# Sparse, block and memory attention: values stationary by column halves, softmax divided ahead of the turn, a new order

## What is computed

```python
# sparse layer: 12 heads, one k and v of 64 columns each for "selected" and "window"
k_cmp = gelu(blocks(k) @ w1) @ w2             # 15 blocks of 32 tokens, stride 16: [15, 2048] @ [2048, 256]; the same for v
o_c = softmax(q @ k_cmp + bias) @ v_cmp
o_s = softmax(q @ k_slc + bias, causal) @ v_slc   # 4 blocks of 64 tokens, top 16: all are selected
o_w = softmax(q @ k_win + bias, causal) @ v_win   # the window is 512: all tokens
o = gate_c * o_c + gate_s * o_s + gate_w * o_w
# block layer: 12 heads with k and v of their own; blocks of 256 tokens, so one block
o = softmax(q @ k + bias, causal) @ v
# both: 4 heads of memory attention (256 memory rows), then
mix = concat(o, o_mem) @ w_out
x = layer_norm(ALPHA * x + mix)
```

## Time and profile before

| | us |
|---|---|
| median of 3 runs | 988.98 (988.08 to 990.57) |
| the profiled execution | 987.35 |
| its span on the core | 985.5 |
| TensorE busy, of the span | 935.0 (95%) |
| VectorE busy | 607.0 (62%) |
| ScalarE busy | 470.5 (48%) |

### The profile page before, as it was taken

How to read it: one execution, slowest core, us unless ns; L and a number is a source line. 1 busy time by engine, 2 the same in 40 slices (tenths; PEclk the granted TensorE clock), 3 DMA queues, 4 the chain that set the end, 5 groups by cost and what they waited for, 6 DMA issues and landing times.

```text
span 985.5 us, 15654 instructions
## 1 busy us (share of the span) xinstructions
PE 935.0 (95%) x6226; PEld 835.4 (85%) x6226; DVE 607.0 (62%) x1108; ACT 470.5 (48%) x833; POOL 37.5 (4%) x72
## 2 busy tenths in 40 slices
PE   8999999699999899889999999998999999999997
PEld 8888978588978777867799999987987889999995
DVE  5669565556566525765786766566444677756565
ACT  5464364355574335652454444434554354444440
POOL 1005100100000100000000000000000000000000
PEclk9999999889999799999999999999999999999999
DMA  8835334264534334212555555546233365555551
GB/s 311 289 129 183 129 108 151 78 219 160 161 107 155 122 117 160 95 43 86 192 173 184 190 180 189 179 171 224 97 108 107 128 203 188 189 174 189 191 192 43
DMA packets 45508, 155.14 MB, mean 157 GB/s; under 512 B 5404, under 2 KB 8060, under 8 KB 45436
## 3 DMA queue, kind: packets, MB, share of 16 engines
q1 hardware_dynamic: 41840, 145.98, 43.2%
q10 hardware_dynamic: 3596, 8.16, 2.9%
HBM read 152.78 MB, written 1.34 MB: 156 GB/s over the span
## 4 chain that ended last, share of the span: by engine, by line
PE 82%; DVE 9%; ACT 6%; issue 2%; POOL 1%; DMA 1%; DVEq 0%; ACTq 0%
PE ps L1933 12%; PE ps L1922 8%; PE ps L1921 8%; PE ps L1920 8%; PE ps L749 6%; PE ps L656 5%; PE ps L657 5%; PE ps L658 5%; PE ps L672 4%; PE ps L861 4%; PE ps L674 4%; PE ps L673 4%; PE ps L828 2%; PE ps L836 2%; ACT sm L896 2%
## 5 line engine op out<-in xcount | busy, mean ns | idle before, releaser
L623 DVE TENSOR_TENSOR wlo<-raw,whi 128x1024 fp32r<-128x1024 f32 (+1 forms) x263 | 313.2, 1215 | 47.8 <-ACT whi L617 47.4
L617 ACT ACTIVATE whi<-raw 128x1024 fp32r<-128x1024 f32 (+1 forms) x263 | 271.4, 1047 | 126.2 <-DMA raw<-in_ws 46.8
L1920 PE MATMUL ps<-thi,whi 128*128 128x256 f32 x640 | 181.2, 283 | 0.0
L1922 PE MATMUL ps<-thi,wlo 128*128 128x256 f32 x640 | 181.1, 283 | 0.0
L1921 PE MATMUL ps<-tlo,whi 128*128 128x256 f32 x640 | 181.1, 283 | 0.0
L1921 PEld LDWEIGHTS ps<-tlo,whi 128*128 128x128 f32 x640 | 122.8, 192 | 0.7
L1920 PEld LDWEIGHTS ps<-thi,whi 128*128 128x128 f32 x640 | 122.8, 192 | 0.7
L1922 PEld LDWEIGHTS ps<-thi,wlo 128*128 128x128 f32 x640 | 122.8, 192 | 0.0
L656 PE MATMUL ps<-thi,whi 128*128 128x256 f32 (+1 forms) x416 | 121.5, 292 | 0.4 <-ACT arena L1542 0.4
L657 PE MATMUL ps<-tlo,whi 128*128 128x256 f32 (+1 forms) x416 | 118.3, 284 | 0.0
L658 PE MATMUL ps<-thi,wlo 128*128 128x256 f32 (+1 forms) x416 | 118.2, 284 | 0.0
(11 more groups left out here) (251 smaller groups left out, 1315.1 us busy)
## 6 DMA issues: line engine op xcount, KB each, us to landing
raw<-in_ws SPq DMA_DIRECT2D x264, 512.0 KB, 4.0
vecs<-in_vecs ACTq DMA_DIRECT2D x12, 512.0 KB, 6.1
raw<-in_ws SPq DMA_DIRECT2D x4, 384.0 KB, 3.9
tb<-brow ACTq DMA_DIRECT2D x8, 192.0 KB, 4.5
rows<-in_mem SPq DMA_DIRECT2D x2, 512.0 KB, 4.2
x<-in_x SPq DMA_DIRECT2D x1, 1024.0 KB, 9.5
out<-x SPq DMA_DIRECT2D x4, 256.0 KB, 2.0
tb<-in_decay SPq DMA_DIRECT2D x1, 768.0 KB, 8.8
```

Source lines behind the costliest of these rows:

```text
L617: a.i.activation(whi[:, j % NSPLIT, 0:n], raw[:, u % NRAW, 0:n], ACT.Copy).then_inc(*a.sig("hi", u))
L623: d.i.tensor_tensor(wlo[:, j, 0:n], raw[:, u % NRAW, 0:n], whi[:, j, 0:n].bitcast(F), ALU.subtract).then_inc(*d.sig("lo", u))
L1920: p.i.matmul(o, wh[:, k, :], thi[:, k, :], start=k == 0, stop=False)
L1922: mm = p.i.matmul(o, wl[:, k, :], thi[:, k, :], start=False, stop=k == 7)
```

## The change

- `w1`: its eight units move to the end of the plan and out of the ring `raw`; ScalarE issues their loads (step `w1load`) into six buffers of their own. The four contraction tiles of a step go to four quarters of 32 output partitions (`blk` widened from 15 to 32 columns); `comp 1` adds the quarters up and turns them with a matmul against `quarters`, and the gelu comes after it.
- Groups of the sparse, block and memory attention get a `mul` step (`dve_scale`): VectorE divides the probabilities by their sum, and multiplies them by the gates, before they are turned; `pe_turn` waits for it.
- `val` (`pe_val_columns`): the value (64 columns) is stationary, the turned probabilities (128 columns) move, side 0 writes output partitions 0 to 63 and side 1 64 to 127. In the sparse stage both branches, and the compressed one by a full matmul, add up in PSUM. The output is already the transposed one that the projection takes.
- `fin` is now the split into high and low part (`act_out`, `dve_out`); `mix`, `cmpo`, and the divisions and sums of `dve_fin` for these groups are gone. `pe_project` waits for `out_lo` of the group.
- New orders of both lists, sparse groups with rows 0 ahead of rows 1; the block stage's half-full group moves from the last place to heads 0 to 3.

```diff
-    w1 = [(nm, k) for nm in "kv" for k in range(4)]
-    for t in range(6):
-        for nm, k in w1[2 * t:2 * t + 2] if t < 3 else ():
-            unit(f"a_w1{nm}", f"a_cmp_w1_{nm}_2", span(0, 256), span(4 * k, 4), split=False)
-        if t == 3:
-            for nm, k in w1[6:8]:
-                unit(f"a_w1{nm}", f"a_cmp_w1_{nm}_2", span(0, 256), span(4 * k, 4), split=False)
-        tiles("a_q", a, span(0, 768), only=(t,))
...
+    for nm in "kv":
+        for k in range(4):
+            unit(f"a_w1{nm}", f"a_cmp_w1_{nm}_2", span(0, 256), span(4 * k, 4), split=False)
...
+    at = ODD.index(("proj", "o", 4, 0))
+    ODD[at:at] = [("w1load", i) for i in range(4)]
...
+        nsa += [nsa_group(0, 4 * i, 4), nsa_group(1, 4 * i, 2), nsa_group(1, 4 * i + 2, 2)]
...
+    NSA = [
+        ("chunk", "a_v", 0, 0), ("chunk", "a_v", 1, 0), ("T", 5, 1), ("w1load", 4), ("chunk", "a_v", 0, 1), ("chunk", "a_v", 1, 1),
+        ("tile", "a_c", 0), ("blocks",), ("tile", "a_c", 1), ("w1", "k", 0), ("tile", "a_qm", 0), ("w1", "k", 1), ("w1load", 5),
+        ("w1", "k", 2), ("w1load", 6), ("tile", "a_qm", 1), ("w1", "k", 3), ("w1load", 7), ("log", m0), ("w1", "v", 0),
+        ("tile", "a_q", 0), ("w1", "v", 1), ("tile", "a_q", 1), ("mul", m0), ("w1", "v", 2), ("w1", "v", 3), ("comp", 0), ("log", m1),
+        ("turn", m0, 0), ("tile", "a_q", 2), ("log", n0), ("mul", m1), ("comp", 1), ("tile", "a_q", 3), ("turn", m0, 1), ("comp", 2),
+        ("turn", m1, 0), ("turn", m1, 1), ("val", m0), ("fin", m0), ("mul", n0), ("tile", "a_q", 4), ("log", n1), ("turn", n0, 0),
+        ("turn", n0, 1), ("comp", 3), ("log", n2), ("tile", "a_q", 5), ("val", m1), ("mul", n1), ("turn", n1, 0), ("mul", n2),
+        ("fin", m1), ("turn", n1, 1), ("log", n3), ("cmp",), ("turn", n2, 0), ("add_x", "a", 0), ("add_x", "a", 1), ("cmp2",),
+        ("proj", "a", 0, 0), ("log", n4), ("cmpt", 0), ("proj", "a", 1, 0), ("log", n5), ("mul", n3), ("proj", "a", 0, 1),
+        ("turn", n2, 1), ("val", n0), ("proj", "a", 1, 1), ("fin", n0), ("proj", "a", 2, 0), ("turn", n3, 0), ("cmpt", 1), ("mul", n4),
+        ("turn", n3, 1), ("val", n1), ("fin", n1), ("val", n2), ("fin", n2), ("turn", n4, 0), ("log", n6), ("mul", n5),
+        ("turn", n4, 1), ("val", n3), ("proj", "a", 3, 0), ("turn", n5, 0), ("proj", "a", 2, 1), ("fin", n3), ("mul", n6),
+        ("proj", "a", 3, 1), ("turn", n5, 1), ("val", n4), ("log", n7), ("fin", n4), ("proj", "a", 4, 0), ("turn", n6, 0), ("log", n8),
+        ("mul", n7), ("proj", "a", 4, 1), ("turn", n6, 1), ("val", n5), ("fin", n5), ("proj", "a", 5, 0), ("val", n6), ("mul", n8),
+        ("fin", n6), ("proj", "a", 5, 1), ("turn", n7, 0), ("turn", n7, 1), ("proj", "a", 6, 0), ("turn", n8, 0), ("turn", n8, 1),
+        ("val", n7), ("proj", "a", 7, 0), ("fin", n7), ("proj", "a", 6, 1), ("norm", "a", 0), ("val", n8), ("fin", n8), ("T", 7, 0),
+        ("proj", "a", 7, 1), ("norm", "a", 1),
+    ]
...
+    moba = [group("moba", 1, evens(0, 4), 0, 4, 0), group("moba", 0, evens(0, 4), 0, 4, 0), group("moba", 1, evens(4, 4), 4, 4, 256),
+            group("moba", 0, evens(4, 8), 4, 8, 256), group("moba", 1, evens(8, 4), 8, 4, 512)]
...
+    after = {2: [("log", m0)], 3: [("log", m1), ("mul", m0)], 4: turn_of(m0) + [("mul", m1)], 5: turn_of(m1) + done(m0) + [("log", g2)],
+             6: done(m1) + [("log", g3), ("mul", g2)], 7: turn_of(g2) + [("mul", g3)], 8: done(g2) + turn_of(g3), 9: done(g3) + [("log", g4)],
+             10: [("mul", g4)], 11: turn_of(g4)}
     MOBA += woven(slots, *[(k, [v]) for k, v in after.items()])
-    MOBA += [("mix", "b", 2), ("add_x", "b", 0), ("log", g6), ("add_x", "b", 1), ("proj", "b", 0, 0), ("proj", "b", 0, 1)] + turn_of(g5)
-    MOBA += [("proj", "b", 1, 0), ("proj", "b", 1, 1)] + done(g5) + turn_of(g6) + [("proj", "b", 2, 0), ("proj", "b", 2, 1)] + done(g6)
-    MOBA += [("proj", "b", 3, 0), ("mix", "b", 3), ("proj", "b", 3, 1)]
+    MOBA += [("log", g5), ("add_x", "b", 0), ("add_x", "b", 1)] + done(g4) + proj("b", 0, 0) + proj("b", 0, 1) + [("log", g6), ("mul", g5)]
+    MOBA += proj("b", 1, 0) + proj("b", 1, 1) + [("turn", g5, 0), ("mul", g6)] + proj("b", 2, 0) + [("turn", g5, 1)] + proj("b", 2, 1) + done(g5)
+    MOBA += turn_of(g6) + proj("b", 3, 0) + proj("b", 3, 1) + done(g6)
...
+    def act_w1_load(a, i):
+
+        if i < 4:
+            a.wait_ge("mix_t", "o", 3)
+        elif i < 6:
+            a.wait_ge("xw", "o", 1, 1)
+        else:
+            a.wait_ge("w1", w1_units[i - 6])
+        at = plan[w1_units[i]]["at"]
+        a.i.dma_start(w1_bufs[i % 6], inp["ws"][at:at + P * UNIT].rearrange("(p n) -> p n", p=P)).then_inc(*a.sig(f"w1raw{i}", "all", by=16))
...
+        if (s, n, q) in gives:
+            p.wait_ge("out_lo", gives[s, n, q].g)
+        else:
+            p.wait_ge("mix_lo", s, n // 2)
...
-        p.wait_ge("mul" if g.kind == "diff" else "exp", g.g)
+        p.wait_ge("mul" if g.scaled else "exp", g.g)
...
+    def pe_val_columns(p, g):
+
+        if g.kind == "nsa":
+            p.wait_ge("pcT", g.q)
+        p.fill(g.out, ("out_hi", g.g), ("out_lo", g.g))
+        z = 2 if g.kind == "nsa" else 1
+        for c in range(len(g.sides[0])):
+            o = c // z * P
+            for y in range(g.nb):
+                k = (c * g.nb + y) * P
+                for s in range(2):
+                    mm = p.i.matmul(ps[64 * s:64 * s + 64, g.out, o:o + P], value(g, s, c, y), g.pts[s][:, k:k + P],
+                                    start=c % z == 0 and y == 0, stop=g.kind != "nsa" and y == g.nb - 1)
+            if g.kind == "nsa" and c % 2:
+                h = g.h0 + c - 1
+                mm = p.i.matmul(ps[:, g.out, o:o + P], N["vbd"][:, h % 4:h % 4 + 2, :].rearrange("p h d -> p (h d)"),
+                                N["pcT"][:, g.q, h // 4 * P:h // 4 * P + P], start=False, stop=True)
+        mm.then_inc(*p.sig("val", g.g))
+
+    def out_tiles(s, g):
+
+        n0 = MIX_ORDER[s].index(g.at // P)
+        for a, b in ((n0, min(n0 + g.n // 2, 4)), (max(n0, 4), n0 + g.n // 2)):
+            if a < b:
+                hi, lo, n = mixed(a)
+                yield ps[:, g.out, (a - n0) * P:(b - n0) * P].rearrange("p (k n) -> p k n", n=P), [
+                    v[:, n:n + b - a, g.q * P:g.q * P + P] for v in (hi, lo)]
+
+    def act_out(a, s, g):
+        a.wait_ge("val", g.g)
+        for src, (hi, _) in out_tiles(s, g):
+            last = a.i.activation(hi, src, ACT.Copy)
+        last.then_inc(*a.sig("out_hi", g.g))
+
+    def dve_out(d, s, g):
+        d.wait_ge("out_hi", g.g)
+        for src, (hi, lo) in out_tiles(s, g):
+            last = d.i.tensor_tensor(lo, src, hi.bitcast(F), ALU.subtract)
+        last.then_inc(*d.sig("out_lo", g.g))
...
+    def dve_scale(d, g):
+
+        n, W = len(g.sides[0]), g.W
+        d.wait_ge("exp", g.g)
+        d.i.reciprocal(g.l, g.l).then_inc(*d.sig("dve"))
+        d.wait_ge("dve")
+        if g.kind == "nsa":
+            d.wait_ge("gate", g.q)
+            gates = N["gte"][:, g.q, 3 * g.h0:3 * g.h0 + 3 * g.n].rearrange("p (i s c) -> p s i c", s=2, c=3)[:, :, :, 1:3]
+            l = g.l.rearrange("p (s i z) -> p s i z", s=2, z=2)
+            d.i.tensor_tensor(l, l, gates, ALU.mult).then_inc(*d.sig("dve"))
+            d.wait_ge("dve")
+        for s in range(2):
+            v = g.slots[s][:, 0:n * W].rearrange("p (c w) -> p c w", c=n)
+            mu = d.i.tensor_tensor(v, v, g.l[:, s * n:s * n + n].unsqueeze(2).to_broadcast([P, n, W]), ALU.mult)
+        mu.then_inc(*d.sig("mul", g.g))
...
-                p.wait_ge(f"raw{u % NRAW}", u)
-                wv = raw[:, u % NRAW, 0:1024].rearrange("p (k n) -> p k n", k=4)
+                i = w1_units.index(u)
+                p.wait_ge(f"w1raw{i}", "all")
+                wv = w1_bufs[i % 6].rearrange("p (k n) -> p k n", k=4)
                 for kl in range(4):
-                    kt = 4 * a[1] + kl
-                    mm = p.i.matmul(ps[0:15, 2, T * z:T * z + T], N["blk"][:, z, kt, :], wv[:, kl, :], start=kt == 0, stop=kt == 15)
+                    mm = p.i.matmul(ps[32 * kl:32 * kl + 32, 2, T * z:T * z + T], N["blk"][:, z, 4 * a[1] + kl, :], wv[:, kl, :],
+                                    start=a[1] == 0, stop=a[1] == 3)
                 mm.then_inc(*p.sig("w1", u))
             elif what == "comp" and a[0] == 1:
...
+                p.wait_ge("quarters", 0)
+                p.fill(2, ("hid", 0))
                 for y in range(4):
-                    t = p.i.transpose(ps[:, 2, 16 * y:16 * y + 15], N["hrow"][0:15, y * P:y * P + P], ident[0:15, 0:15])
-                t.then_inc(*p.sig("hidt", 0))
+                    mm = p.i.matmul(ps[:, 2, 16 * y:16 * y + 16], N["hrow"][:, y * P:y * P + P], quarters[:, 0:16], start=True, stop=True)
+                mm.then_inc(*p.sig("hidt", 0))
```

More of the change, by code:

```diff
@@ L294, in _build @@
     nhalf = sb("nhalf", [P, 8])
+    quarters = sb("quarters", [P, 32])
     AW = 9728
@@ L370, in _build @@
     split_no = {u: j for j, u in enumerate(split_units)}
```

(43 more changed lines are left out.)

151 lines of the change are left out of this document (60 added, 91 removed).

## The result

| | before | changed |
|---|---|---|
| median, us | 988.68 (988.08 to 990.57) | 964.16 (961.63 to 967.14) |
| ratio | | 0.975 [0.972, 0.978] |
| span of the profiled execution | 985.5 | 959.8 |

A forecast was written before the change was run, and what follows sets the result against it. TensorE was taken to bound both stages. Sparse stage - 18.4 us of work and + 4.2 of idle, block stage - 5.8, together - 20.0: span 985.5 to 965.5, median 969.0 us, range 956 to 985.

The forecast's parts named there:

- Overlap of column halves and quarters: Values and w1: matmuls run side by side; values save 8.4 us (sparse) and 4.9 us (block), w1 9.4 us.
- Rival (c): Values and w1: 32-bit halves by columns don't overlap, so both cost more; 992.5 us at its middle; chance 0.13.
- (d): Values and w1: two at a time where four are meant, pairs gain half; 979 us; chance 0.16 together with Rival (b).
- The drain at a change of mode: TensorE, value and w1 steps: changing between whole and halved array costs about 0.2 us; if free, about 5 us better.
- Work taken off: Sparse stage, TensorE: values - 8.4, w1 - 9.4, mix - 1.7, comp 1 + 0.5, branch sum + 0.6: - 18.4 us.
- Idle time: Sparse stage, TensorE: of 8.1 us idle, 1.8 goes with the mix, 4 and 2 come: + 4.2 us.
- With VectorE 85 to 90% busy: Sparse stage's second half: VectorE has 44 to 47 us of 52, so 4 us of TensorE idle allowed.
- rival (a): Both stages: no chain comes late, idle falls to the 2 us before the last transposes; 957 us; chance 0.14.
- the forecast's own sign: Sparse stage: TensorE idle 10 to 15 us, some released by the scale's line, 2 us before the last transposes.
- The tail: Sparse stage's end: the last transposes wait for the norm with little other work beside it, 2 us of idle.
- Block stage: Block stage: values - 4.9 and mix - 1.7 us of work, + 0.8 us for turns close behind their logits: - 5.8.
- Rival (b): Sparse stage's second half: VectorE sets it, 52 us stretch to 60; 979 us; chance 0.16 together with (d).

The follow-up runs named there:

- run 1: Changed kernel with side 0's value matmuls all ahead of side 1's (per pair of cells in the sparse layer): 968.42 us, ratio 0.975.
- run 2: Changed kernel with the four matmuls of one w1 step writing the same output quarter one after another: 974.02 us, ratio 0.980.
- run 5: Changed kernel with one more multiply-sized VectorE instruction in each of the 18 groups' normalization: 969.12 us, ratio 0.979.
- e9: Changed kernel in a plain order, three groups between logits and turn, each scale ahead of the newest logits: 1004.86 us, ratio 1.014.
- run 3: Changed kernel with the sparse list's second half in plain order: 992.61 us; with one group more between logits and turn, and turn and values: 999.65 us.
- e10: As e9, but a group's two turns are set apart by the value products of the group before: 988.41 us, ratio 0.998.
- e4: Kernel before with only w1's quarters and what belongs to them, weights still in the ring: 993.58 us, ratio 1.002.
- e8: As e4, with identity products in the two TensorE gaps that it opened: 989.02 us, ratio 0.997.
- e2: Changed kernel with each w1 step's four matmuls writing a single quarter, step k quarter k: 974.02 us, ratio 0.980.
- e1: Changed kernel with the value matmuls of the two sides one side after the other, not alternating: 968.42 us, ratio 0.975.

## Why the prediction was right, point by point

- **Overlap of column halves and quarters.** Right, and right in size: values 1.03 us for a forecast 1.07, w1 4.3 us in all for 4.8 (14.2 before). Taking the logits' halves by rows as the nearest row was the choice that carried the forecast. Rival (c) is out by run 1; (d) is out by the step times of 1.03 and 0.57 us, and by run 2.
- **The drain at a change of mode.** Forecast at 0.2 us from the logits. Value step: 1.03 less 4 x 0.218 (two records 0.109 us apart) leaves 0.16 us. In the rows 0 groups, with four changes, the two halves cost 1.17 us where one run costs 1.03. This agrees with the Trainium skill ("TensorEngine Tiling (Array Packing)", Key Properties), which says that changing the mode drains TensorE.
- **Work taken off.** Forecast 18.4 us for the sparse stage; TensorE's busy time fell by 16.0, from 117.1 to 101.1. From start to next start w1 gave 9.9 us, the values 8.3 and the mix 1.9, `comp 1` cost 0.6 and the sum of the branches 1.7 (forecast 0.6): 17.8. The missing 1.8 us lies mostly in steps that were to stay as they were: the projections take 24.2 us for 23.1, the turned sides 10.8 for 10.4. In the new order the projections stand in shorter runs, and the first one behind another kind of step takes 0.54 to 0.58 us, one behind a projection 0.45 to 0.47.
- **Idle time: the term that was mis-sized.** Forecast 12.3 us in the sparse stage (8.1, less 1.8, plus 4 and 2), measured 5.8. Of the 6.5 us, 1.7 are the new waits (4.3 for 6), and 4.8 the old ones: I let 6.3 of the 8.1 us stay, and 1.5 stayed. The view of TensorE's waits in the kernel before, 346.98 to 472.3 us, has three rows at steps that the change takes away or moves (us in total, times, longest):

```profile
PE ps L836 <- DVE r L735: 2.8, 2, 1.8
...
PE ps L1663 <- ACT arena L1751: 1.0, 1, 1.0
...
PE ps L724 <- DVE rows L1843: 0.8, 1, 0.8
```

The mix and `cmpo` take 3.6 us with them and not 1.8, since two waits ended with L735 and one with L1843. The wait for the gelu (1.0) and two more of 0.9 and 0.5 us went with the order; of 2.1 us for copies of turned sides 1.5 are left. VectorE's load in the whole stage was foreseen well (75 us and 68%; measured 72.7 and 68%), but its second half was 40 us of 57.7, 69%, and not 44 to 47 of 52: "With VectorE 85 to 90% busy" did not come about. In all, 6.5 us of idle less than forecast and 2.4 us of busy time more: the stage gained 18.3 for 14.2. The two errors have opposite signs, and that part of the agreement is luck. With 6.9 us idle in both stages the kernel lies nearer to rival (a), which had 2, than to the forecast's 16.6; the forecast's own sign, 10 to 15 us of idle in the sparse stage, was not met.
- **The tail.** 1.25 us for 2.
- **Block stage.** - 7.9 for - 5.8. Its idle time fell by 2.4 us, where I had added 0.8.
- **Rival (b), VectorE sets the second half.** Out by run 5: even 7.6 us more of VectorE's work added 2.7. The Trainium skill warns ("TensorEngine Tiling (Array Packing)", PSUM Bottleneck) that the copies out of PSUM may become the bottleneck once TensorE is faster. In the changed order they aren't; in e9 they are the longest wait (21.3 us), by their place in ScalarE's queue and not by their length, 0.6 us each.
- **Missing from the forecast.** How much hangs on the order, which I costed at nothing but idle time in VectorE's chain: in the plain orders of run 3 the same instructions are 28 us and more slower. The prediction had no step that told a good order from a plain one. And the granted clock between the layers: I held the stages' 1.00 for safe, which was right in them, and did not see the 2.2 us in front of the block stage. That 1.7 us came back ahead of the sparse stage is luck too.

## What to carry to other kernels

Plain 32-bit matmuls with 64 or 32 stationary columns are worth putting side by side on column halves or quarters, alternating in the queue: 1.8 to 1.0 us for eight, 3.55 to 1.0 for two w1 steps. Here an edit that takes TensorE's work away paid only where the order kept scales, exponentials and copies out of each other's queues: ask of every step what stands ahead of it on VectorE and on ScalarE, and don't turn two sides through one bank back to back (e10 against e9: 16.5 us). Where TensorE is the bound and waits some microseconds at a fixed place, products of the identity in that gap can keep its clock at full speed: here 8.9 us for 66 of them.

## What the hardware did that I had not expected

- **The granted clock fell behind some idle gaps and not behind others.** In the changed kernel's profile it fell behind those of 3.84, 6.02, 1.33 (with 2.35 us more idle behind it) and 2.76 us, and stayed at 1.00 behind 2.15, 1.30 and 1.25 us. Behind 3.84 us idle (178 to 182) it was 0.58 from 183 to 187 us; filled, 1.00. In the kernel before it stayed at 1.00 behind 2.75 us idle ahead of the block stage. The Trainium skill ("TensorE: Matmul & The Clock Gate", HAM oscillation) tells the same of gaps in which TensorE waits for data: it slows down for the work behind each. The traces agree for the gaps of 3.84 and of 5.64 and 6.02 us in both kernels; of the shorter ones, some did it and some didn't.
- **It can stay down while TensorE is busy.** In e4 it was 0.50 for 20 us with TensorE busy for all 20, with logits, narrow value products and transposes; in e8 the same work ran at 1.00. Why it came back at 430 us isn't shown.
- **Matmuls on another quarter start ahead of earlier ones.** Two w1 steps side by side in e2, each in one quarter, took 2.73 us and not 3.7. By the record starts in the trace the second step begins at 355.05, 0.64 us before the first step's last record (355.69, the one that signals the step's end): about two matmuls of each run at the same time, across the border of the steps. In e1 the border of the two sides shows the same.
